# First pooling layer: the 16-column sums in fp32 on GpSimd instead of matmuls; sample states through array tiles and one longer stream

## The chip, the cores and the metric

One Trainium2 chip, 8 cores, the same program on each: every core takes one prompt of the batch and 16 of the 128 sample sequences. There is no communication between cores. The metric is the device time of the slowest core in microseconds.

## The reference, cut to what matters

One step of a two-layer trunk, layer 0 with a pooling mixer and layer 1 with a retention mixer, each followed by a SwiGLU FFN (D_MODEL 1024, D_FF 2816), over 2064 prompt positions (16 meta tokens and 2048) and one new token for each sample.

```python
# layer 0, four groups of 256 channels, windows w = 2, 4, 8, 16
s = cs[:, end, sl] - cs[:, start, sl]          # sum over the trailing w rows
diff = (s / cnt - xn).astype(xn.dtype)
mixed = einsum('btgc,gcd->btgd', diff, w_pool) * pool_scale
# layer 1, sample group, one token: for each of 4 heads, state (256, 512)
s_new = gamma * s0 + k^T v
o = q s_new                                    # then GroupNorm, gate, w_out
```

The new states of the samples (16 samples x 4 heads x 256 x 512 fp32 a core, 32 MB) are read from and written to HBM.

## The kernel before

Activations lie with channels on the partitions and tokens along the free dimension. The tokens are done in two halves: half 0 has 1056 columns (16 samples, 16 meta tokens, 1024 prompt tokens) in tile `hA`, half 1 has 1024 columns (and the 16 sample columns, carried over) in `hB`. A column block is 352 wide (`BW`); the first pooling layer works in four blocks, `FIRST`, of 176, 176, 352 and 352 columns, whose inputs are loaded one after the other (each load waits for the one before, the last for the first FFN weights too).

The stages in order of time: pooling layer of half 0 (`p0_*`), FFN 0 of half 0, retention layer of half 0 (`ret_layer(0)`), FFN 1 of half 0, FFN 0 of half 1, retention layer of half 1, FFN 1 of half 1. The second pooling layer (`p1_steps`) and the recurrent states of the samples (`sample_steps`) are no stages of their own: they are "streams" (`S.add`), lists of steps that are put between the steps of a main stage in proportion to its cost. `S.finish` puts in what is left of a stream. In the program before, heads 0 and 1 of the samples are a stream of FFN 1 of half 0, heads 2 and 3 of FFN 0 of half 1.

**Order on each engine.** The program order gives the dependences (through keys of tiles and PSUM banks). A planner (`Prog.arrange`) then puts the operations of each engine in an order by list scheduling with a cost for each operation, and each engine runs its order strictly. The four PSUM banks `pb` are a ring handed out in program order, so an operation that gets a bank in the program waits until the one four banks before has been read out, wherever the planner would like it. `sx`, `po` and the two banks of `psU` are outside the ring.

**The first pooling layer, `p0_block(b)`** (L713, the line of all matmuls; L722 `tensor_tensor`; L725 `scalar_tensor_tensor` on VectorE; L729 copies and L733 activations on ScalarE). `p0_x` writes the normalised input in bf16 (`hB`), eight VectorE instructions. `p0_group` sums a window of w columns by w matmuls a channel tile, each with an identity times 1/w (the first with 1/w - 1) and the input shifted by k columns, all into one `pb` bank; ScalarE copies it out. `p0_out` multiplies with the pooling weights and adds to `hA`. Then the norm of FFN 0 follows, and its first matmuls, `pb<-xn,wring`, take the next banks of the ring.

**The samples, a unit for each sample and head.** `U` has four slots of 128 x 1024 fp32, one state each. `unit_a` loads the state of two units ahead (DMA on the SP queue), spreads the sample's row of v over 128 partitions by a matmul with the selector `sel` (`psU<-vx,sel`), and adds k v to the state with two VectorE instructions. `unit_b` casts the state to bf16 (`snb`, ScalarE), scales it by gamma in place (ScalarE), stores it (SP queue), and multiplies the cast state of the unit before with the masked q (`po<-snb,qm`, two matmuls of 128 stationary columns, of which 16 matter). After 16 units the head's output is normalised and gated.

**Weights** come by DMAs from the GpSimd queue (L157, `wring`), with a wait for each where its ring space is not yet free; the first five each wait for the one before.

**The retention layer** computes q, k, v (`main_qkv`) and the gate (`main_g`) head by head, with the recurrent chunks of a head as a stream beside (`chunk_steps`), which use `U`, `psU`, `po` and `sx` too.

## Time and profile before

| | |
|---|---|
| device time, three runs | 1668.44, 1672.44, 1797.84 us (median 1672.44) |
| the profiled execution | 1670.36 us |
| its span, slowest core (core 4) | 1668.8 us |
| spans of the eight cores | 1657.7 to 1668.8 us |
| granted TensorE clock, eight cores | 0.992 to 0.996 |
| busy: TensorE, VectorE, ScalarE, GpSimd | 1620.6, 868.1, 669.9, 542.3 us |
| moved by DMA | 201.31 MB, 121 GB/s over the span |

All times of the prediction's argument are of the one profiled execution. The span is from the first to the last instruction of the slowest core; the device time of the same execution is 1.6 us longer.

### The profile page before, as it was taken

What the parts mean: (1) busy time and instruction counts of PE and PEld (TensorE: products, weight loads), DVE (VectorE), ACT (ScalarE), POOL (GpSimd) and SP (SyncE); (2) the same over time, 40 slices, a digit from 0 to 9 for tenths busy, and PEclk for the clock granted to TensorE, in tenths of its full rate; (3) what the DMA queues carried; (4) which work ended last, traced back from release to release, by engine and by line L of the source; (5) the groups of instructions that cost most, each with busy time, mean ns of one, the idle gap of its engine ahead of it and who ended that gap; (6) DMA issues with size and microseconds to landing.
All of it is one profiled execution on the core that took longest, in us unless ns stands there. A gap on an engine that the chain in (4) does not pass through costs nothing.

```text
span 1668.8 us, 32601 instructions; the slowest of 8 cores (1657.7 to 1668.8 us)
## 1 busy us (share of the span) xinstructions
PE 1620.6 (97%) x10945; PEld 1038.4 (62%) x10945; DVE 868.1 (52%) x1651; ACT 669.9 (40%) x1165; POOL 542.3 (32%) x830
## 2 busy tenths in 40 slices
PE   6999999999999999999999999999999999999997
PEld 5666666555565665666665665665655656666666
DVE  4622222855655663889283354448556566422225
ACT  4621022354433554544373544555543345310123
POOL 3000001557747631222140210025677475000002
PEclk9999999999999999999999999999999999999999
DMA  6634434243235466686678987976443241543422
GB/s 156 157 52 85 83 67 82 52 77 64 39 64 102 77 160 176 181 217 158 159 196 209 242 215 213 246 199 190 77 102 59 58 100 27 114 76 56 91 46 103
DMA packets 55745, 201.31 MB, mean 121 GB/s; under 512 B 6688, under 2 KB 21024, under 8 KB 45840
## 3 DMA queue, kind: packets, MB, share of 16 engines
q0 software_dynamic: 15840, 103.82, 35.4%
q1 hardware_dynamic: 39600, 95.07, 16.5%
q8 instruction: 92, 1.51, 0.4%
q14 instruction: 69, 0.57, 0.1%
q10 hardware_dynamic: 144, 0.35, 0.1%
HBM read 256.69 MB, written 47.25 MB: 182 GB/s over the span
## 4 chain that ended last, share of the span: by engine, by line
PE 87%; DMA 5%; issue 2%; ACT 2%; POOL 2%; DVE 2%; DVEq 0%; POOLq 0%; ACTq 0%; SPq 0%
PE pb L713 78%; PE po L713 4%; DMA U<-sret 3%; PE psU L713 2%; PE sx L713 2%; PE sx L717 1%; DMA hB<-xT 1%; DMA nrs<-U 1%; ACT rstd L733 0%; POOL hC L722 0%; DMA cf_sb<-cf 0%; DVE xn L725 0%; POOL aff L722 0%; POOL stt L722 0%; ACT L733 0%
## 5 line engine op out<-in xcount | busy, mean ns | idle before, releaser
L713 PE MATMUL pb<-xn,wring 128*128 128x352 bf16 (+3 forms) x5856 | 936.3, 308 | 12.0 <-ACT sg L733 7.0
L713 PEld LDWEIGHTS pb<-xn,wring 128*128 128x128 bf16 x5856 | 564.5, 98 | 308.0 <-issue 19.1
L713 PE MATMUL pb<-hC,wring 128*128 128x352 bf16 (+4 forms) x2576 | 425.4, 307 | 1.2 <-DVE hB L722 1.2
L722 DVE TENSOR_TENSOR hC<-pb,sg 128x352 bf16<-128x352 f32 (+3 forms) x270 | 136.5, 508 | 373.0 <-PE pb L713 346.9
L713 PEld LDWEIGHTS pb<-hC,wring 128*128 128x128 bf16 x2576 | 249.6, 98 | 124.3 <-issue 2.0
L733 ACT ACTIVATE sg<-pb 128x352 bf16<-128x352 f32 (+3 forms) x270 | 120.4, 451 | 461.7 <-PE pb L713 452.2
L713 PE MATMUL pb<-wring,xn 128*128 128x512 bf16 (+1 forms) x544 | 163.2, 379 | 0.0
L157 POOL DMA_DIRECT2D wring<-w_gu x44 | 24.5, 556 | 418.0 <-PE pb L713 389.0
L722 DVE TENSOR_TENSOR hB<-pb,hB 128x352 f32<-128x352 f32 (+4 forms) x152 | 73.8, 495 | 95.0 <-PE pb L713 94.0
L725 DVE SCALAR_TENSOR_TENSOR U<-psU,ksf,U 128x512 f32<-128x512 f32 x128 | 94.9, 747 | 21.3 <-DMA U<-sret 9.1
L722 DVE TENSOR_TENSOR hA<-pb,hA 128x352 f32<-128x352 f32 (+1 forms) x144 | 72.7, 513 | 63.9 <-PE pb L713 63.2
L729 ACT CAST snb<-U 128x1024 bf16<-128x1024 f32 x64 | 66.5, 1039 | 79.0 <-DVE U L725 55.9
L725 DVE SCALAR_TENSOR_TENSOR U<-U,psU 128x1024 f32<-128x1024 f32 x64 | 78.0, 1218 | 30.4 <-PE psU L713 19.9
L713 PEld LDWEIGHTS pb<-wring,xn 128*128 128x128 bf16 (+1 forms) x544 | 51.8, 98 | 50.3 <-issue 6.4
L722 POOL TENSOR_TENSOR aff<-aff,cf_sb 128x512 f32<-128x512 f32 (+1 forms) x68 | 67.5, 993 | 47.7 <-DVE aff L722 43.5
L722 POOL TENSOR_TENSOR accb<-accb,sq 128x352 f32<-128x352 f32 (+1 forms) x72 | 62.4, 867 | 62.3 <-ACT sq L733 46.2
L729 ACT CAST U<-U 128x1024 bf16<-128x1024 f32 x64 | 66.7, 1042 | 39.3 <-DVE U L725 29.9
L1194 ACT ACTIVATE on<-po,stt 128x512 bf16<-128x512 f32 (+1 forms) x68 | 52.8, 777 | 71.7 <-POOL stt L1188 38.4
L157 POOL DMA_DIRECT2D wring<-w_d x32 | 17.3, 541 | 178.2 <-PE pb L713 178.2
L733 ACT ACTIVATE U<-U 128x1024 f32<-128x1024 f32 x64 | 67.6, 1056 | 5.7 <-ACT snb L729 0.4
L722 DVE TENSOR_TENSOR aff<-sx,cf_sb 128x512 f32<-128x512 bf16 (+1 forms) x68 | 45.0, 662 | 38.7 <-PE sx L717 23.4
L1183 DVE BATCH_NORM_STATS2 stt<-po 128x6 f32<-128x512 f32 (+1 forms) x68 | 47.3, 695 | 27.0 <-PE po L713 23.6
(147 smaller groups left out, 1703.4 us busy)
## 6 DMA issues: line engine op xcount, KB each, us to landing
wring<-w_gu POOLq DMA_DIRECT2D x44, 1024.0 KB, 10.2
U<-sret SPq DMA_DIRECT2D x64, 512.0 KB, 5.9
nrs<-U SPq DMA_DIRECT2D x64, 512.0 KB, 5.5
wring<-w_in POOLq DMA_DIRECT2D x24, 1024.0 KB, 9.7
wring<-w_d POOLq DMA_DIRECT2D x16, 768.0 KB, 7.8
wring<-w_d POOLq DMA_DIRECT2D x16, 640.0 KB, 10.4
wring<-w_out POOLq DMA_DIRECT2D x8, 1024.0 KB, 10.6
hA<-xT SPq DMA_DIRECT2D x2, 1408.0 KB, 13.9
```

What stands on the lines that cost most here:

```text
L157: h.dma_start(out=o_ap, in_=i_ap).then_inc(sem, 16)
L713: return P.op('pe', lambda h: h.matmul(out, lhsT=lhsT, rhs=rhs, start=start, stop=stop), reads=reads, writes=writes, cost=passes * max(_fr ...
L717: return P.op('pe', lambda h: h.transpose(out, in_, ident), reads=reads, writes=writes, cost=max(_free(out), 64) / 2.4 + 1.3)
L722: return P.op(eng, lambda h: h.tensor_tensor(out=out, in0=a, in1=b, op=op), reads=reads, writes=writes, cost=cost)
L725: return P.op('dve', lambda h: h.scalar_tensor_tensor(out=out, in0=a, scalar=s, in1=b, op0=op0, op1=op1), reads=reads, writes=writes, cost ...
L729: return P.op('act', lambda h: h.copy(out=out, in_=in_), reads=reads, writes=writes, cost=130 + 0.93 * _free(out))
L733: return P.op('act', lambda h: h.activation(out=out, in_=in_, func=func, bias=bias, scale=scale), reads=reads, writes=writes, cost=160 + 0 ...
L1183: dve(lambda h: h.bn_stats(out=s[0:n, 0:6], in_=po[0:n, :]), [pok], [sk], 690)
L1194: act(lambda h: h.activation(out=on[0:n, :], in_=po[0:n, :], func=ACT.Identity, bias=s[0:n, 9:10], scale=s[0:n, 8:9]), [pok, sk], [onk], 777)
```

## The change

1. In the first pooling layer, the group with window 16 (channel tiles 6 and 7) no longer goes through matmuls. Its normalised input is kept in fp32 in scratch tiles `XF` (which share the memory of the rotary table `cs`), with 16 columns of the block before in front, copied by GpSimd. GpSimd sums by doubling, four additions a tile (steps 1, 2, 4, 8), and VectorE forms sum/16 minus input. The two tiles share the scratch `XF[2]` and `XF[3]`.
2. As `cs` is scratch at first, its load moves from behind the input loads to behind the pooling layer.
3. The sample units go in pairs and fours. v's row is also copied to partitions 32 to 63 (one more ScalarE copy a head), and one operation of the tensor engine spreads two samples with two matmuls of 32 rows each, in two row tiles of the array. The output is formed for four samples at once by eight matmuls of 32 stationary columns, in four column tiles. `snb` has four buffers for it; the selector `sel` and its GpSimd instruction are gone. The GroupNorm of the samples then runs over 128 partitions, and its transposes over 128 columns in place of 16.
4. The stream of the samples starts beside head 3 of the first retention layer (four units, of which the states lie in `hC`), and the remaining 60 units are one stream over both FFNs and the q, k, v step of head 0 of the second retention layer.

```diff
@@ first pooling layer (G_SUM is 3)
-            for c in range(8):
+            for c in range(2 * G_SUM):
                 stt(B.b(c, 0, c0, n), A.f(c, c0, n), ...)
+            for c in range(2 * G_SUM, 8):
+                X, xkk = XF[c - 6], [('XF', c - 6)]
+                x0 = 0
+                if b:
+                    m = FIRST[b - 1][1] - (32 if b == 1 else 0)
+                    pcopy(X[:, 0:16], X[:, m:m + 16], xkk, xkk)
+                    x0 = 16
+                stt(X[:, x0:x0 + n], A.f(c, c0, n), w32[...], r[:, o:o + n], ALU.mult, ALU.mult, ..., xkk)
...
+                if g >= G_SUM:
+                    X, xkk = XF[c - 6], [('XF', c - 6)]
+                    src, sk, sh = X, xkk, 1
+                    while sh < w:
+                        i = 2 if src is X or src is XF[3] else 3
+                        dst, dk = XF[i], [('XF', i)]
+                        lo = 2 * sh
+                        tt('pool', dst[:, lo:16 + n], src[:, lo:16 + n], src[:, lo - sh:16 + n - sh], ALU.add, sk, dk)
+                        src, sk = dst, dk
+                        sh *= 2
+                    stt(B.b(c, 1, c0, n), src[:, 16:16 + n], 1.0 / w, X[:, 16:16 + n], ALU.mult, ALU.subtract, ...)
+                    continue
@@ the load of cs: from behind the input loads to behind the pooling layer
-        csl = P.dma('sp', [(cs[:, 0, :], csd[0, :, 0:NA]), ...], semkey='cs', after=xl[3:4])
...
         wrel(wprec)
+        P.dma('sp', [(cs[:, 0, :], csd[0, :, 0:NA]), ...], writes=csk, semkey='cs')
@@ samples, two units
+                        if (h, b) != (0, 2):
+                            s_load(16 * h + b + 2 + i)
+                    def spread(e):
+                        for i in range(2):
+                            p = slice(32 * i, 32 * i + 32)
+                            ins = e.matmul(psU[:, i, :], lhsT=identb[p, 32*i+b+i:32*i+b+i+1].to_broadcast([32, 128]),
+                                           rhs=vx[h][p, :], start=True, stop=True)
+                    P.op('pe', spread, ..., cost=290)
@@ samples, four units
+                        for c in range(2):
+                            for j in range(4):
+                                w0 = 17 * (b + j) - b // 4
+                                ins = e.matmul(po[32 * j:32 * j + 32, :], lhsT=qm[:, c, w0:w0 + 32], rhs=snb[j][:, c, :],
+                                               start=b == 0 and c == 0, stop=b == 12 and c == 1)
+                    P.op('pe', dots, ..., cost=650)
@@ v of the samples, twice
                     acopy(o[0:n, :], pb[0:n, :], [pk], ok)
+                    if t == 8:
+                        acopy(o[n:2 * n, :], pb[0:n, :], [pk], ok)
@@ the streams
+        first4, sw = sw[0:7], sw[7:]
+        ret_layer(0, A, 'R0', 32, NA, norm_after(A, C_NF1, 'F01'), first4)
...
-        s01 = S.add(sample_steps(0, True) + sample_steps(1, False), 0.97 * fcost)
+        ss = S.add(sw, 2 * fcost + 8 * 8 * NB + 8 * 8 * 512)
...
-        s23 = S.add(sample_steps(2, False) + sample_steps(3, False), 0.97 * fcost)
...
+        ret_layer(1, B, 'R1', 0, NY, norm_after(B, C_NF1, 'F11'), ss)
@@ in ret_layer
             main_qkv(0)
+            if half == 1:
+                S.finish(beside)
...
+                side = S.add(beside, 2.2 * span) if h == 3 and half == 0 else None
                 main_g(h)
+                if side:
+                    S.finish(side)
```

## Rows read from the trace of the kernel before

**Rows 1.** The page: busy time, share of the span, instructions.
```profile
PE 1620.6 (97%) x10945; PEld 1038.4 (62%) x10945; DVE 868.1 (52%) x1651; ACT 669.9 (40%) x1165; POOL 542.3 (32%) x830
```
**Rows 2.** Windows by stage: length, busy us (instructions) by engine, clock, DMA share, GB/s.
```profile
0.00:100.00 100.00, 82.62 (x667) 62.60 (x668) 54.59 (x128) 48.11 (x126) 19.96 (x42) 0.97 0.57 131
100.00:310.00 210.00, 210.00 (x1410) 137.68 (x1409) 60.87 (x113) 39.40 (x83) 24.79 (x36) 1.00 0.41 74
...
866.00:1128.00 262.00, 252.81 (x1670) 163.05 (x1669) 123.56 (x225) 130.46 (x182) 33.18 (x51) 0.99 0.86 218
```
**Rows 3.** Windows of 10 us in which the tensor engine stands idle or slow.
```profile
880.00:890.00 10.00, 7.84 (x51) 4.70 (x48) 2.90 (x5) 1.34 (x3) 0.00 (x0) 1.00 0.99 281
...
1000.00:1010.00 10.00, 6.39 (x32) 3.34 (x31) 4.10 (x7) 3.87 (x4) 0.00 (x0) 0.83 0.89 294
...
1040.00:1050.00 10.00, 7.51 (x51) 4.38 (x49) 4.11 (x10) 9.15 (x12) 1.80 (x5) 1.00 0.84 255
1050.00:1060.00 10.00, 10.00 (x58) 6.22 (x57) 7.05 (x14) 6.32 (x8) 1.19 (x2) 0.83 0.90 211
```
**Rows 4.** Timeline, VectorE then TensorE, 1000 to 1007 us: start, us, instruction, idle before.
```profile
1004.25 2.26 DVE L725 SCALAR_TENSOR_TENSOR U<-psU,ksf,U 128x512 f32<-128x512 f32 x3 [3.68 <-DMA U<-sret]
...
1006.00 0.58 PE L713 MATMUL psU<-vx,sel 128*128 128x512 bf16 x1 [3.61 <-DVE U L725]
```
**Rows 5.** Groups by shape, TensorE: the matmuls that the change removes or replaces.
```profile
L713 PE MATMUL po<-snb,qm 128*128 128x512 bf16 x128 | 43.0, 383 | 0.2 <-ACT on L1194 0.2
L713 PE MATMUL psU<-vx,sel 128*128 128x512 bf16 x64 | 24.1, 384 | 3.6 <-DVE U L725 3.6
L713 PE MATMUL pb<-hB,snb 128*128 128x352 bf16 x120 | 22.4, 325 | 0.4 <-DVE hB L725 0.2
```
**Rows 6.** Timeline, TensorE: unbroken runs of 352 and of 512 columns.
```profile
105.74 19.55 PE L713 MATMUL pb<-xn,wring 128*128 128x352 bf16 x130
...
325.43 2.54 PE L713 MATMUL pb<-wring,xn 128*128 128x512 bf16 x11
327.80 0.31 PE L713 MATMUL pb<-xn,wring 128*128 128x352 bf16 x1
```
**Rows 7.** Timeline, TensorE, 366 to 369 us: stationary tiles of 32 between 128 columns.
```profile
366.70 1.04 PE L713 MATMUL pb<-wring,xn 128*32 128x512 bf16 x4
367.67 0.39 PE L713 MATMUL po<-hC,U 128*128 128x512 bf16 x1
367.99 0.71 PE L713 MATMUL pb<-wring,xn 128*32 128x512 bf16 x2
368.54 0.38 PE L713 MATMUL po<-U 128*128 128x512 bf16 x1
368.76 0.39 PE L717 MATMUL sx<-identb,on 128*128 128x128 bf16 x4
369.07 0.71 PE L713 MATMUL pb<-wring,xn 128*32 128x512 bf16 x2
```
**Rows 8.** Timeline, GpSimd, first 60 us.
```profile
35.73 0.59 POOL L157 DMA_DIRECT2D wring<-w_gu  x1 [13.00 <-DMA wring<-w_gu]
36.74 0.76 POOL L722 TENSOR_TENSOR xn<-hA 128x352 bf16<-128x352 f32 x1 [0.42 <-DMA hA<-xT]
46.53 0.59 POOL L157 DMA_DIRECT2D wring<-w_gu  x1 [9.03 <-DMA wring<-w_gu]
49.42 1.13 POOL L722 TENSOR_TENSOR xn<-hA 128x352 bf16<-128x352 f32 x1 [2.30 <-DMA hA<-xT]
```
**Rows 9.** Timeline, VectorE, 57 to 75 us: last block's input and last residual additions.
```profile
57.20 0.58 DVE L725 SCALAR_TENSOR_TENSOR hB<-hA,w,rstd 128x352 bf16<-128x352 f32 x1
...
72.85 1.08 DVE L725 SCALAR_TENSOR_TENSOR hA<-pb,cf_sb,hA 128x352 f32<-128x352 f32 x2 [1.95 <-PE pb L713]
```
**Rows 10.** Timeline, TensorE: the first FFN matmuls.
```profile
70.80 0.24 PE L713 MATMUL pb<-xn,wring 128*128 128x176 bf16 x1
```
**Rows 11.** Groups by shape, GpSimd: fp32 additions.
```profile
L722 POOL TENSOR_TENSOR accb<-accb,sq 128x352 f32<-128x352 f32 x48 | 42.2, 879 | 50.8 <-ACT sq L733 41.5 <-ACT accb L733 5.5 <-ACT snb L729 0.4
```
**Rows 12.** DMA issues, 866 to 1128 us: count, KB each, median us to landing.
```profile
U<-sret SPq DMA_DIRECT2D x33, 512.0 KB, 6.9
nrs<-U SPq DMA_DIRECT2D x33, 512.0 KB, 6.4
```

176 lines of the change are left out of this document (95 added, 81 removed).

## The prediction

> **What bounds the kernel now.** First the page's busy line: the tensor engine is busy for 1620.6 us of 1668.8, so it bounds nearly everywhere, and some 48 us are left in which it stands idle [rows 1]. Then the windows by stage, to see where those are: 17.4 us of them in the first 100 us, none in the FFN that follows, 9.2 us in the FFN of the second half [rows 2]. A change can therefore gain in two ways: matmul time that is taken away where the engine is never short of work, or a wait that goes. Time taken away where it waits for something else gains nothing.
>
> What the engine waits for differs by stage. In the second half's FFN the windows of 10 us show it at 7.84, 6.39 and 7.51 us busy, while the DMA engines are 0.84 to 0.99 busy, and twice a clock of 0.83 [rows 3]; the granted clock has two levels, 2.4 and 1.2 GHz, and a mean of 0.83 is a third of the window at the lower one, which costs half of that, 1.7 us. Idle and clock together are 2.2 + 3.6 + 1.7 + 2.5 + 1.7 = 11.7 us. The timeline names the cause of the largest: VectorE waits 3.68 us for a state of a sample (`U<-sret`), and the tensor engine, which must run its order, stands behind it for 3.61 us before it may spread the next v [rows 4].
>
> The first 70 us are another thing. The last input block is there at 49.4 us, where GpSimd starts on it [rows 8]; its normalised input begins at 57.2 us, and its last residual additions end at 73.9 us [rows 9]. The FFN's matmuls begin at 70.8 us [rows 10], though their first weights landed at 35.7 us, where GpSimd's wait for them ends [rows 8]: the ring of four `pb` banks holds them back until the last banks of the pooling layer are read out. So FFN matmuls cannot fill holes in the pooling layer, and what matters is the end of the last block's chain.
>
> **The window sums.** Removed are 64 matmuls of 352 columns (blocks 2 and 3), 32 of 176 and 32 of 144. An unbroken run gives the pace: 130 of 352 columns in 19.55 us, 0.149 us each [rows 6]; by columns the small ones cost 0.075 and 0.061. The sum is 9.5 + 2.4 + 2.0 = 13.9 us of tensor engine time, and eight ScalarE copies. (The group's mean of 325 ns [rows 5] contains the pipeline's depth and is not a price.) That is the upper end, if nothing new stands in the way.
>
> Something does. In their place stand, a block, eight dependent GpSimd additions. The trace has the same addition at 128x352 in fp32 for 0.88 us [rows 11]; the same shape of product took 0.76 us once and 1.13 us beside busy engines [rows 8]. With about 0.13 us between dependent instructions a chain of eight is 8.1 us, by 1.13 us 10.1. For block 3: input at about 56.7 us (in the old order 57.2, first of the eight now), chain to 65.5 with the copies in front, 1.1 us more for the halo's two instructions on the same queue, two VectorE instructions of 0.6 us partly beside it, then two pairs of matmuls and two additions, 2 us: about 69 us where before it was 73.9. Meanwhile the tensor engine has 28 window matmuls (4.2 us) and the other groups' outputs, and the ring lets through only the FFN step whose banks come before group 3. Gain 5 us. Block 2 needs no more: its chain starts at 44 us and ends before block 3's input is normalised. Bounds: 9 us gained if the chain ends at 65 because the additions take 0.76 us, and 5 us lost if GpSimd's queue is held (a rival, below).
>
> The Trainium skill speaks against this step: "GPSIMD Engine Reference", section Engine selection, says elementwise additions on a tile belong on VectorE and cost about twice as much on GpSimd; VectorE, a little over half busy there, would by that rule do the chain in about 4 us and end some 3 us earlier. The sum above does not use it.
>
> **The load of `cs`** (1 MB) leaves the DMA engines free from 49 to 59 us, where only weights for later steps come in, and lies afterwards in a stage with DMA share 0.41 in which the tensor engine has no idle time [rows 2]. It is read 200 us later. Nothing.
>
> **The samples' array tiles.** Before, a unit has one matmul of 512 columns to spread v and two for the output, 192 in all [rows 5]. Their pace is (327.80 - 325.43) / 11 = 0.216 us [rows 6], so they cost 41.5 us. They lie among the FFNs' matmuls, where the engine is otherwise busy, so a saving counts in full. After, there are 32 pairs and 16 operations of eight. If tiles run side by side, a pair lasts 0.216 us and the eight two times 0.216. No row shows two tiles together. But rows show what it costs to go to a narrower tile and back: four matmuls with 32 stationary columns occupy 366.70 to 367.67, that is 0.97 us in place of 4 x 0.216 = 0.86; the one of 128 columns behind them 0.32 in place of 0.22; the next two 0.55 in place of 0.43 [rows 7]. Each change of tile shape costs 0.11 us, 0.22 for in and out again. And the matmuls of a group can hardly start at the same moment: four transposes behind one another start in (0.31 - 0.11) / 4 = 0.05 us steps [rows 7]. So a pair costs 0.216 + 0.22 = 0.44, with one step 0.49, I take 0.46; the eight cost 0.43 + 0.22 = 0.65, with three steps 0.80, I take 0.72. Sum: 32 x 0.46 + 16 x 0.72 = 14.7 + 11.5 = 26.2 us, a gain of 15.3 us. Lower price 24.5 (gain 17), higher 28.5 (gain 13); with changes of shape hidden 13.8 (gain 27.7); with tiles one after the other 64 x 0.216 + 128 x 0.216 + 48 x 0.22 = 52.1, a loss of 10.6.
>
> That a change of tiling mode drains the engine is what the Trainium skill says in "TensorEngine Tiling (Array Packing)", Key Properties; the trace agrees, with 0.11 us. "TensorE: Matmul & The Clock Gate", Part 3, reports four row tiles with K = 32 at 3.07 times one after another, not 4; by that the eight would cost 8 x 0.216 / 3.07 = 0.56 us and the change of shape, which is inside my two ends.
>
> **The longer stream.** In the second half's FFN 33 units are loaded and 33 stored [rows 12]. The new stream has 60 units over 1,179,648 columns of work, of which an FFN has 540,672, so 27.5 units fall into each FFN, four into the retention layer before and five into the q, k, v step after. That takes 5.5 loads and stores of 0.5 MB, 5.5 to 6 MB, from a stage that moves 218 GB/s x 262 us = 57 MB, and puts them where the DMA engines are less busy. A tenth less traffic, and 9 us of distance a unit in place of 8. Every unit still has the same four slots and loads come only two units ahead, so the delays get rarer and don't vanish: I take half of the 11.7 us, 6, with bounds 0 and 11.7.
>
> **What is added.** Four ScalarE copies, hidden beside q, k, v; 16 transposes of 128 columns for 16 of 16, at 0.05 us steps under 1 us; four units beside head 3 in the first retention layer, where the chunks share `psU`; five units beside the rotary products, and the load of head 0's state, which now waits for a sample's store. VectorE and ScalarE are half busy [rows 1], the queues behind them have other matmuls to cover. I put 2 us on all of it, bounds 0 and 6.
>
> **Sum.** -5 - 15.3 - 6 + 2 = -24.3 us. Against the profiled execution 1670.36 - 24.3 = 1646.1, its span 1644.5; the median of the runs is 2.1 us above it, so **1648 us**.
>
> **Rivals.**
> - **GpSimd is held by the weights.** Its queue runs in order, and in this stretch it stood 13.0 and 9.0 us for a weight DMA before issuing the next [rows 8]. The planner estimates the landing; if it puts additions of blocks 1 or 2 behind such an issue, they end at 46.5 or later and all outputs, and by the ring of banks the next block, move. For: the waits are there today. Against: the additions are critical and ready earlier, so they should be put in front. Price: the last block ends 5 us later than before instead of 5 earlier, 1658 us.
> - **The tiles don't run side by side.** The groups then cost 52.1 us: -5 + 10.6 - 6 + 2 = +1.6, **1674 us**, slower than before. It decides from the point where the groups cost more than 41.5 + 9 = 50.5 us, 3.2 us for four units; half overlap isn't enough for it. For: no row shows two tiles at once. Against: the tiles are disjoint in the array and write disjoint banks or partitions.
> - **The late states go altogether**: 11.7 instead of 6, and the lower price of the tiles: -5 - 17 - 11.7 + 2 = -31.7, 1641 us. For: the busiest stage is relieved. Against: the same slots and distance.
> - **Changes of shape are hidden** behind other matmuls: -5 - 27.7 - 6 + 2 = -36.7, 1636 us. Against: in rows 7 each one shows.
>
> **How the numbers follow.** Chances: forecast 0.50 (own range 1641 to 1656), held GpSimd 0.20, late states gone 0.14, hidden changes of shape 0.07, serial tiles 0.09. The range 1632 to 1664 leaves out the serial tiles and the ends of others. Within 2% means 1639 to 1706 us, about what a measurement of this kernel can tell from no change. Below lie the hidden changes of shape and a part of the late-states case and of the forecast with the prologue's upper bound: 0.19 faster. Slower by over 2% needs several losses together: 0.03. The same: 0.78.
>
> **What the changed profile would show.** Right: `po` matmuls with 32 stationary columns whose eight take 0.65 to 0.8 us until the next 128-column matmul starts; `psU` pairs 0.44 to 0.49; the first FFN matmul at 66 to 69 us and the last pooling addition near 69; fewer idle windows from 866 to 1060; no new idle time in the retention layers. Wrong: GpSimd additions behind a weight issue of 10 us, the first FFN matmul after 71 us, eight `po` matmuls over 1.7 us, or a tensor engine that waits for `XF` sums with its clock at half for longer than before.

## The result and the profile after

| | before | changed |
|---|---|---|
| device time, median (range) | 1670.76 us (4 runs) | 1646.72 us (1644.68 to 1764.9, 4 runs) |
| ratio | 1 | 0.9855, 95% interval [0.9836, 0.9875] |
| span of the profiled execution | 1668.8 us | 1643.8 us (core 4, as before) |

The 1764.9 us is an execution in which the cores of one die had a lower clock, and it is not in the ratio. The change gives 24 us, 1.5%: within the 2% band, and 1 us from the 1648 predicted. The sum was right; how it is made up was not (the errors of its terms cancelled), and most of what follows is about that.

The page's busy line of the changed kernel:

```profile
PE 1589.3 (97%) x10817; PEld 1010.3 (61%) x10817; DVE 881.9 (54%) x1671; ACT 663.3 (40%) x1157; POOL 561.9 (34%) x867
```

Its windows by stage (columns as in [rows 2]):

```profile
0.00:100.00 100.00, 74.72 (x555) 53.44 (x556) 65.37 (x138) 45.90 (x119) 40.15 (x79) 0.97 0.57 131
...
866.00:1128.00 262.00, 256.77 (x1759) 163.29 (x1758) 136.55 (x251) 126.33 (x186) 47.50 (x67) 0.99 0.88 222
```

Against [rows 1] the tensor engine is busy for 31.3 us less (1620.6 to 1589.3); the 13.9 us of window matmuls and the 18.1 us worked out below make 32.0. Against [rows 2] its idle time in the first 100 us rose from 17.4 to 25.3 us, while VectorE went from 54.59 to 65.37 us busy: of 13.9 us of window matmuls 7.9 came back as waiting. From 866 to 1128 us the idle time fell from 9.2 to 5.2 us.

**The pooling layer.** Timeline of the changed kernel, GpSimd, the last block's sums:

```profile
60.33 4.23 POOL L721 TENSOR_TENSOR cs_sb<-cs_sb 128x366 f32<-128x366 f32 x4 [0.44 <-DVE cs_sb L724]
65.09 0.82 POOL L721 TENSOR_TENSOR cs_sb<-cs_sb 128x366 f32<-128x366 f32 x1 [0.53 <-DVE cs_sb L724]
67.18 2.81 POOL L721 TENSOR_TENSOR cs_sb<-cs_sb 128x364 f32<-128x364 f32 x3 [1.27 <-DVE hB L724]
```

VectorE, its last residual additions:

```profile
71.26 1.08 DVE L724 SCALAR_TENSOR_TENSOR hA<-pb,cf_sb,hA 128x352 f32<-128x352 f32 x2
```

TensorE, the first FFN matmul ([rows 10]):

```profile
68.30 0.24 PE L712 MATMUL pb<-xn,wring 128*128 128x176 bf16 x1 [0.17 <-issue]
```

Eight additions take from 60.33 to 69.99 us, 9.7 us. By themselves they are as priced, 0.89 us each in the mean and 0.14 us apart; but twice the chain waits for VectorE (1.27 us for the instruction that reads a scratch tile before it may be overwritten, 0.53 for the next product). The last residual additions end at 72.3 us, where [rows 9] has 73.9.

What became of VectorE shows in the groups by shape, first 110 us (instructions, busy us, mean ns, idle time). The kernel before:

```profile
L725 DVE SCALAR_TENSOR_TENSOR hB<-hA,w,rstd 128x352 bf16<-128x352 f32 x16 | 8.3, 580 | 2.5 <-ACT rstd L733 2.5
```

The changed kernel:

```profile
L724 DVE SCALAR_TENSOR_TENSOR hB<-hA,w,rstd 128x352 bf16<-128x352 f32 x12 | 10.5, 910 | 0.0
...
L724 DVE SCALAR_TENSOR_TENSOR cs_sb<-hA,w,rstd 128x352 f32<-128x352 f32 x4 | 3.5, 879 | 0.2 <-ACT rstd L732 0.2
...
L724 DVE SCALAR_TENSOR_TENSOR hA<-pb,cf_sb,hA 128x352 f32<-128x352 f32 x16 | 8.6, 574 | 0.1
```

The product of two SBUF inputs went from 580 to 910 ns; the addition of the same size whose first input is PSUM stayed (582 ns before, 574 now). The mean of 910 ns hides what happens to each. Timeline, VectorE: a product with no addition beside it, and two that start in one:

```profile
42.64 0.58 DVE L724 SCALAR_TENSOR_TENSOR cs_sb<-hA,w,rstd 128x352 f32<-128x352 f32 x1 [0.21 <-ACT rstd L732]
...
61.09 0.62 DVE L724 SCALAR_TENSOR_TENSOR hB<-hA,w,rstd 128x352 bf16<-128x352 f32 x1
61.63 1.11 DVE L724 SCALAR_TENSOR_TENSOR hB<-hA,w,rstd 128x352 bf16<-128x352 f32 x1
```

GpSimd, the additions in which they start:

```profile
60.33 0.99 POOL L721 TENSOR_TENSOR cs_sb<-cs_sb 128x366 f32<-128x366 f32 x1 [0.44 <-DVE cs_sb L724]
61.47 0.89 POOL L721 TENSOR_TENSOR cs_sb<-cs_sb 128x364 f32<-128x364 f32 x1
```

The first of the two starts late in its addition and takes 0.62 us, the second early in its own and takes 1.11; both end 0.38 us after the addition does. In the single records the same holds, at 0.38 us, for all twelve products of the last two blocks that start inside an instruction of GpSimd with SBUF inputs (durations from 0.62 to 1.26), while the four that start in none take 0.57 to 0.59. So such a product gets nowhere until the addition is done. In windows of 10 us VectorE is by then full (7.30 and 7.62 busy before):

```profile
45.00:55.00 10.00, 7.77 (x38) 3.84 (x36) 10.00 (x14) 5.19 (x13) 6.91 (x9) 0.83 0.96 233
55.00:65.00 10.00, 8.50 (x50) 4.22 (x50) 9.93 (x18) 6.43 (x15) 5.54 (x8) 1.00 0.39 69
```

**The tiles.** Timeline of the changed kernel, TensorE, a group of eight output matmuls and what follows:

```profile
710.65 0.62 PE L1311 MATMUL po<-snb,qm 128*32 128x512 bf16 x8
711.20 1.17 PE L712 MATMUL pb<-hC,wring 128*128 128x320 bf16 x7
```

The second four of these eight:

```profile
710.87 0.39 PE L1311 MATMUL po<-snb,qm 128*32 128x512 bf16 x4
```

The same, a pair that spreads v:

```profile
657.59 0.39 PE L1273 MATMUL psU<-vx,identb 32*128 32x512 bf16 x2
657.91 0.46 PE L712 MATMUL pb<-xn,wring 128*128 128x320 bf16 x2
```

Eight matmuls of 512 columns in 0.55 us, two in 0.32, from start to the next one's start. On the way in each costs 0.09 us more: the matmul of 320 columns ahead of it started 0.23 us before it (at 710.42 and at 657.36), where the step between two such is 0.14 (657.22 to 657.36). In sum that is 0.64 and 0.41 us, where one after another they would take 1.73 and 0.43 by the pace of [rows 6]. The second four start 0.22 us behind the first, which is the pace of a single matmul, and the last four take 0.32 us until the next shape starts, 0.10 of it for the change. In the single records the matmuls of a group of four start 3 to 4 ns apart in most cases; the steps of 0.05 us that the prediction took over from transposes aren't there. For all: 16 x 0.64 + 32 x 0.41 = 23.4 us in place of 41.5, 18.1 us of work saved.

**The stream.** DMA issues of the changed kernel, 866 to 1128 us ([rows 12]):

```profile
U<-sret SPq DMA_DIRECT2D x33, 512.0 KB, 8.2
nrs<-U SPq DMA_DIRECT2D x32, 512.0 KB, 7.1
```

Timeline, TensorE, its longest wait for a state's `psU` there ([rows 4]):

```profile
988.18 0.61 PE L1273 MATMUL psU<-vx,identb 32*128 32x512 bf16 x2 [2.45 <-DVE U L724]
```

As many loads and one store less, and DMA share 0.88 as against 0.86. But this is a window of time and not the stage: the FFN 0 of half 1 ends at 1138 us before and at 1108 us now (its last `pb<-hC,wring`, core 4), so that the window now holds a part of the q, k, v step as well. Counted by the stage (871 to 1138 us before, 862 to 1108 us now) there are 31 loads and 30 stores in place of 35 and 34, and 54.2 MB in place of 59.0. The stage has also become 21 us shorter, so the DMA share is 0.88 as against 0.86 and the rate 220 as against 221 GB/s: less is moved, in less time. The longest such wait shrank from 3.61 to 2.45 us.

### The profile page after: what moved, and what is told of

Same layout as the page of the kernel before. It is cut to its first block, busy times and chain, and to the rows that moved or that the text cites. A ratio compares the mean times of both kernels' runs of the same rounds, so it can differ in the third digit from the quotient of the medians.

```text
span 1643.8 us, 32354 instructions; the slowest of 8 cores (1630.2 to 1643.8 us)
## 1 busy us (share of the span) xinstructions
PE 1589.3 (97%) x10817; PEld 1010.3 (61%) x10817; DVE 881.9 (54%) x1671; ACT 663.3 (40%) x1157; POOL 561.9 (34%) x867
## 4 chain that ended last, share of the span: by engine, by line
PE 87%; DMA 5%; DVE 4%; issue 2%; ACT 2%; POOL 1%; DVEq 0%; POOLq 0%; SPq 0%; ACTq 0%
PE pb L712 78%; PE po L712 3%; PE sx L712 2%; PE psU L712 2%; PE sx L716 1%; DMA hA<-xT 1%; DMA U<-sret 1%; DMA hB<-xT 1%; DVE xn L724 1%; DVE hB L724 1%; DMA nrs<-U 1%; PE psU L1273 1%; DVE hA L721 1%; POOL hC L721 0%; ACT L732 0%
## 5 line engine op out<-in xcount | busy, mean ns | idle before, releaser
L712 PE MATMUL pb<-xn,wring 128*128 128x352 bf16 (+3 forms) x5856 | 915.1, 308 | 7.8 <-ACT sg L732 4.5
L712 PE MATMUL pb<-hC,wring 128*128 128x352 bf16 (+4 forms) x2576 | 412.8, 307 | 1.2 <-DVE hB L721 1.2
L712 PE MATMUL pb<-wring,xn 128*128 128x512 bf16 (+1 forms) x544 | 156.0, 379 | 0.0
L724 DVE SCALAR_TENSOR_TENSOR U<-psU,ksf,U 128x512 f32<-128x512 f32 x120 | 89.0, 746 | 19.3 <-PE psU L1273 8.9
L1214 ACT ACTIVATE on<-po,stt 128x512 bf16<-128x512 f32 x68 | 52.8, 777 | 82.6 <-POOL stt L1208 56.5
L728 ACT CAST snb<-U 128x1024 bf16<-128x1024 f32 x60 | 62.3, 1039 | 53.7 <-DVE U L724 41.2
L1203 DVE BATCH_NORM_STATS2 stt<-po 128x6 f32<-128x512 f32 x68 | 47.3, 696 | 38.9 <-PE po L712 20.9
L732 ACT ACTIVATE U<-U 128x1024 f32<-128x1024 f32 x60 | 63.3, 1056 | 4.7
## 6 DMA issues: line engine op xcount, KB each, us to landing
wring<-w_in POOLq DMA_DIRECT2D x24, 1024.0 KB, 10.5
wring<-w_out POOLq DMA_DIRECT2D x8, 1024.0 KB, 10.5
hA<-xT SPq DMA_DIRECT2D x2, 1408.0 KB, 11.6
```

Source lines behind the costliest of these rows:

```text
L712: return P.op('pe', lambda h: h.matmul(out, lhsT=lhsT, rhs=rhs, start=start, stop=stop), reads=reads, writes=writes, cost=passes * max(_fr ...
L724: return P.op('dve', lambda h: h.scalar_tensor_tensor(out=out, in0=a, scalar=s, in1=b, op0=op0, op1=op1), reads=reads, writes=writes, cost ...
L728: return P.op('act', lambda h: h.copy(out=out, in_=in_), reads=reads, writes=writes, cost=130 + 0.93 * _free(out))
L732: return P.op('act', lambda h: h.activation(out=out, in_=in_, func=func, bias=bias, scale=scale), reads=reads, writes=writes, cost=160 + 0 ...
L1203: dve(lambda h: h.bn_stats(out=s[0:n, 0:6], in_=po[0:n, :]), [pok], [sk], 690)
L1214: act(lambda h: h.activation(out=on[0:n, :], in_=po[0:n, :], func=ACT.Identity, bias=s[0:n, 9:10], scale=s[0:n, 8:9]), [pok, sk], [onk], 777)
```

## The experiments

All ratios are to the kernel before on the same chip, with 95% intervals; the chips differ between groups of runs. From each profile I also read two numbers on all eight cores: when GpSimd issues the fifth FFN weight (the FFN's first matmul lies 38.5 to 40.4 us before it on the eight cores of before, changed, e5, e6, e7 and e9, so this is the pooling layer's end plus nearly a constant), and what is left of that core's span behind it. Medians over the eight cores:

| kernel | ratio | fifth weight, us | the rest, us |
|---|---|---|---|
| before | 1 | 108.5 | 1554.4 |
| before, other order (r3) | 0.9983 [0.9966, 0.9999] | 108.5 | 1551.5 |
| changed | 0.9855 [0.9836, 0.9875] | 106.2 | 1532.2 |
| changed again (r1) | 0.9880 [0.9855, 0.9905] | 105.0 | 1534.2 |
| changed, other order (r2) | 0.9871 [0.9849, 0.9892] | 104.6 | 1531.5 |
| sums alone (e9) | 0.9986 [0.9973, 0.9999] | 104.8 | 1553.4 |
| sums and tiles, old streams (e2) | 0.9945 [0.9925, 0.9966] | 104.9 | 1550.8 |
| sums and long stream, full matmuls (e3) | 0.9900 [0.9865, 0.9936] | 105.1 | 1545.9 |
| all, but serial tiles (e4) | 0.9938 [0.9915, 0.9961] | 103.0 | 1552.5 |
| tiles and stream, matmul sums (e1) | 0.9940 [0.9921, 0.9959] | 115.0 | 1536.2 |
| the same, `cs` load at its old place (e6) | 0.9939 [0.9923, 0.9955] | 117.2 | 1535.7 |
| sums on VectorE (e5) | 0.9947 [0.9925, 0.9969] | 110.2 | 1542.5 |
| one tile on GpSimd (e7) | 0.9872 [0.9857, 0.9888] | 112.0 | 1529.0 |
| squares on ScalarE (e8) | 0.9892 [0.9870, 0.9913] | 105.5 | 1540.7 |

### e1: the sums as matmuls again

```diff
-        G_SUM = 3
+        G_SUM = 4
```

> The changed kernel with its first part undone: the window of 16 goes through matmuls again, tiles and stream stay. Theory (the sums are worth what the first 110 us show, where the fifth FFN weight is issued at 107.9 us after the change and at 110.3 before): 2.4 us slower than the changed kernel, 1649 us, and that weight issued near 110.3 us. Rival (all 13.9 us of removed matmul time count somewhere): 1660 us. Second rival (the sums on GpSimd cost as much as they give): 1647 us.

Measured: 0.9940, fifth weight at 115.0 us. By the ratio that is 1661 us, the first rival's time, but it is no clean undo. Without scratch tiles nothing holds the late `cs` load back, and it was issued on SP's queue at 1.57 us, ahead of `sp_prev` and the second input block. Timeline of e1, TensorE:

```profile
19.27 6.98 PE L712 MATMUL po<-cf_sb,hC 128*128 128x16 f32 x32 [4.48 <-DMA hC<-sp_prev]
```

What follows: a megabyte put in front of the inputs costs a wait of 4.5 us; of the sums it tells nothing that can be separated.

### e2: the old two streams, with pairs and tiles

```diff
-        ss = S.add(sw, 2 * fcost + 8 * 8 * NB + 8 * 8 * 512)
+        s01 = S.add(sample_steps(0, True) + sample_steps(1, False), 0.97 * fcost)
...
+        s23 = S.add(sample_steps(2, False) + sample_steps(3, False), 0.97 * fcost)
```

> The changed kernel with its last part undone: the samples are two streams again, heads 0 and 1 in FFN 1 of half 0, heads 2 and 3 in FFN 0 of half 1, in pairs and with array tiles as changed. Theory (the longer stream is worth the idle and slow-clock time that went between 606 and 1128 us, 14.6 - 13.6 us of idle time and 3.4 us of clock): 4 us slower than the changed kernel, 1651 us, with idle windows and a clock under 1.00 back around 880 to 1060 us. Rival (those went because units go in pairs, and the stream's length does nothing): 1647 us. Second rival (the work put beside the retention layers costs more than it gives): 1644 us or less.

Measured: 0.9945, a loss well over the 4 us expected. The stalls that I expected to come back before 1128 us are the smaller part of it (on core 3 the idle time from 606 to 1128 us is 15.2 us as against 11.6 in the changed kernel, by the windows below). Timeline of e2, TensorE, core 3, the end of the second stream:

```profile
1143.11 1.05 PE L1305 MATMUL po<-snb,qm 128*32 128x512 bf16 x8 [5.07 <-ACT snb L728]
1147.83 0.59 PE L716 MATMUL sx<-identb,on 128*128 128x128 bf16 x4 [3.67 <-ACT on L1214]
```

The same place in e9:

```profile
1136.48 3.48 PE L1304 MATMUL po<-snb,qm 128*128 128x512 bf16 x8 [2.56 <-ACT snb L728]
1143.60 0.25 PE L716 MATMUL sx<-identb,on 16*128 16x16 bf16 x4 [3.63 <-ACT on L1214]
```

A stream that must be done at the FFN's end shows its tail: the last four states' casts, the group norm, the transposes and the gate come one behind the other, and nothing else is left to run. Before, with single units, TensorE was idle for 3.7 us from 1128 to 1405 us on core 3; e9, which differs there by the grouping, has 10.5.

### e3: matmuls 128 wide, with the new stream

```diff
-                                w0 = 17 * (b + j) - b // 4
-                                ins = e.matmul(po[32 * j:32 * j + 32, :], lhsT=qm[:, c, w0:w0 + 32], rhs=snb[j][:, c, :],
+                                w0 = 16 * (b + j)
+                                ins = e.matmul(po[:, :], lhsT=qm[:, c, w0:w0 + 128], rhs=snb[j][:, c, :],
```

> The changed kernel with full-width matmuls for the samples: a pair is spread by two matmuls over all 128 rows, four samples' outputs by eight matmuls of 128 stationary columns, at the same places. Theory (tiles count in full): 41.4 us of matmuls for 23.3 us, 18 us slower, 1665 us. Rival (the engine has slack where they lie, or more overlaps than the tensor engine alone): less than 10 us slower, under 1657 us.

### e4: the same shapes in one tile

```diff
-                                ins = e.matmul(po[32 * j:32 * j + 32, :], lhsT=qm[:, c, w0:w0 + 32], rhs=snb[j][:, c, :],
+                                ins = e.matmul(po[0:32, :], lhsT=qm[:, c, w0:w0 + 32], rhs=snb[j][:, c, :],
```

> The changed kernel with the same tile shapes, but all matmuls of a group in the same tile of the array: both of a pair in rows 0 to 31, all eight of the output in columns 0 to 31. Theory (the gain is that tiles run side by side, and shape changes cost 0.1 us): a pair takes 0.41 + 0.22 = 0.63 us, eight take 8 x 0.216 + 0.2 = 1.94 in place of 0.64, together 32 x 0.22 + 16 x 1.3 = 27.8 us slower than the changed kernel, 1674 us, slower than the kernel before all changes. Rival (a narrow matmul is cheaper by itself): 1647 to 1660 us.

Measured: e3 0.9900, e4 0.9938. Timeline of e4, TensorE, core 3:

```profile
711.30 1.90 PE L1311 MATMUL po<-snb,qm 128*32 128x512 bf16 x8
713.14 2.14 PE L712 MATMUL pb<-hC,wring 128*128 128x320 bf16 x14
```

In one tile the eight take 1.84 us, in four tiles 0.55; a pair 0.53 (657.88 to 658.41) as against 0.32. That is 16 x 1.29 + 32 x 0.21 = 27.4 us more TensorE work, the 27.8 of the expectation; yet the kernel is only 0.9938 - 0.9869 = 0.0069 slower than the changed one (mean of its three ratios), 11.5 us. With e3 it is 18.1 us more work (the price of 41.5 less 23.4) and 0.0031, 5 us, with an uncertainty about as large. So tiles do run side by side, and less than half of what they save reaches the end: e3 meets its rival (under 10 us slower) and e4 has the time of its rival, though not its reason, since a narrow matmul in one tile isn't cheaper. Where it goes is seen in windows over the two FFNs with the states and over the retention layer behind them, on core 3 of each kernel. (The windows are the same in time; in a faster kernel the last part of each already belongs to the next stage.) Before:

```profile
606.00:1128.00 522.00, 510.77 (x3401) 331.20 (x3400) 304.36 (x565) 262.30 (x390) 108.60 (x184) 0.99 0.82 203
1128.00:1405.00 277.00, 273.34 (x1814) 164.11 (x1812) 172.88 (x325) 129.64 (x213) 183.78 (x271) 1.00 0.40 84
```

Changed:

```profile
606.00:1128.00 522.00, 510.44 (x3519) 327.38 (x3518) 317.40 (x591) 251.63 (x389) 122.05 (x198) 1.00 0.79 197
1128.00:1405.00 277.00, 272.93 (x1834) 164.31 (x1833) 168.99 (x325) 137.08 (x221) 170.46 (x257) 1.00 0.41 90
```

e3:

```profile
606.00:1128.00 522.00, 519.12 (x3470) 337.63 (x3471) 314.18 (x577) 249.23 (x383) 114.49 (x193) 1.00 0.79 198
1128.00:1405.00 277.00, 274.58 (x1844) 168.15 (x1843) 169.12 (x323) 130.67 (x213) 173.28 (x260) 1.00 0.39 81
```

e4, the first of the two:

```profile
606.00:1128.00 522.00, 514.46 (x3406) 324.52 (x3404) 305.96 (x556) 243.38 (x379) 112.95 (x190) 1.00 0.78 193
```

e9:

```profile
606.00:1128.00 522.00, 516.73 (x3456) 335.41 (x3455) 317.45 (x581) 265.45 (x395) 114.04 (x190) 1.00 0.82 206
1128.00:1405.00 277.00, 266.50 (x1760) 160.11 (x1757) 162.57 (x312) 125.63 (x207) 173.06 (x259) 0.98 0.34 72
```

e2:

```profile
606.00:1128.00 522.00, 506.82 (x3474) 323.04 (x3472) 318.44 (x592) 258.56 (x394) 116.93 (x194) 0.99 0.81 204
1128.00:1405.00 277.00, 261.92 (x1734) 157.51 (x1732) 160.89 (x308) 126.53 (x205) 173.73 (x260) 0.97 0.37 82
```

Window less busy is idle. In both stages together: before 14.9 us, changed 15.6, e3 5.3, e9 15.8, e2 30.3. From e3 to the changed kernel tiles take 18.1 us of work away and 10.3 of them come back as idle time; with the old streams (e9 to e2) 14.5 do. (Over the eight cores e3 has 5.3 to 11.7 us, median 8.6, and the changed kernel 13.0 to 18.0, median 15.6.) From before to changed the idle time stays as it was, but only as a balance: the longer stream by itself takes 10.5 us of it away (e9 to e3), and the tiles bring 10.3 back.

What TensorE waits for then, core 3, 606 to 1128 us (us in total, times, longest). The changed kernel:

```profile
PE pb L712 <- ACT sg L732: 3.7, 3, 2.1
PE sx L712 <- DVE dfb L724: 3.0, 2, 1.9
...
PE psU L1273 <- DVE U L724: 1.1, 1, 1.1
```

e3:

```profile
PE sx L712 <- DVE hB L724: 1.4, 1, 1.4
...
PE pb L712 <- ACT sg L732: 0.2, 1, 0.2
```

Only 1.1 us is for a state (1.1 to 3.2 on cores 0, 1, 5 and 7). The rest is for the FFN's own activation (`sg`, ScalarE) and for instructions of VectorE for the second pooling layer (`dfb`) and the FFN. So the time comes back as waits for ScalarE and VectorE, which do the FFN's work and the states' in one queue each; which of their instructions make these late no run shows.

### r1, r2, r3: the changed kernel again, and both in another order

The planner breaks ties by a seed; r2 and r3 have another.

```diff
-default_rng(1)
+default_rng(2)
```

> The changed kernel as it is, beside the next ones on one chip. The four kernels before it each undid one part and lost 7.5 to 15 us by their ratios, 51 us in all, where all parts together gained 24. Theory A (the planner's order is worth several us, and each undoing also lost a good order): ratio 0.985 again, about 1647 us. Theory B (the comparison was off by the chip): a ratio of 0.990 or more here.

> The changed kernel with another seed of the planner's random rounds and nothing else: the same instructions in another order on each engine. Theory A (order is worth several us): 5 to 12 us slower than the changed kernel, ratio 0.988 to 0.993. Theory B (the parts are worth what their undoing cost): ratio within 0.002 of the changed kernel's.

> The kernel before with another seed of the planner's random rounds and nothing else. Theory A: differs from the kernel before by 3 to 12 us in either direction (ratio 0.993 to 1.007, outside 0.998 to 1.002). Theory B: ratio 0.998 to 1.002.

Measured: 0.9880, 0.9871, 0.9983. r1 lies between its two theories; r2 and r3 met theory B. The same kernel on another chip moved by 0.0025, 4 us, and another order by a seed by no more than that (r3 by 0.0017, 3 us). A seed doesn't explain that the undos e1, e2 and e3 together lose 30 us of a gain of 22. No undo was run with another seed.

### e5: the doubling sums on VectorE

```diff
-                        tt('pool', dst[:, lo:16 + n], src[:, lo:16 + n], src[:, lo - sh:16 + n - sh], ALU.add, sk, dk)
+                        tt('dve', dst[:, lo:16 + n], src[:, lo:16 + n], src[:, lo - sh:16 + n - sh], ALU.add, sk, dk)
```

> The changed kernel with the doubling sums on VectorE in place of GpSimd. Beside the GpSimd sums VectorE's products of two SBUF inputs took 0.91 us where they take 0.58 alone, while those with a PSUM input stayed at 0.57, and VectorE is 96 to 100% busy from 35 to 65 us: the first layer is now bound by VectorE. Theory (the two engines share access to SBUF): those products go back to 0.58 us, some 9 us of VectorE time in the first 110 us, against 32 additions there of 0.25 to 0.52 us, 13 us: the fifth FFN weight is issued within 2 us of 107.9. Rival (the length of the chain on GpSimd bounds, not VectorE): the chain of a block shrinks from 9.6 to about 4.5 us and that weight is issued 4 us earlier, near 104. The whole within the uncertainty of the planner's order.

Measured: 0.9947, fifth weight at 110.2, 4 to 6 us later than with GpSimd. On core 4 it is at 111.4: neither the theory's 107.9 nor the rival's 104, since an addition takes 0.52 to 0.59 us at these widths and not 0.25 to 0.52. Groups by shape of e5, VectorE, first 110 us:

```profile
L724 DVE SCALAR_TENSOR_TENSOR hB<-hA,w,rstd 128x352 bf16<-128x352 f32 x12 | 6.9, 614 | 0.0
...
L721 DVE TENSOR_TENSOR cs_sb<-cs_sb 128x364 f32<-128x364 f32 x4 | 2.4, 594 | 0.2
```

A window of e5:

```profile
55.00:65.00 10.00, 7.08 (x41) 3.43 (x40) 9.79 (x20) 6.31 (x15) 2.30 (x5) 1.00 0.88 206
```

Two things follow. The stretching of the products (0.91 us) is due to the additions on GpSimd: with the same products and no such additions there it is 0.61. And an addition is in fact quicker on VectorE (0.52 to 0.59 us in the means by shape, as against 0.84 to 0.99 on GpSimd in the changed kernel), but VectorE has no room for it. (The rest of the run is 8 to 11 us longer than in the changed kernel, in stages that the edit doesn't touch; of that below, at e8.)

### e6: matmul sums, and the `cs` load at its old place

```diff
-        G_SUM = 3
+        G_SUM = 4
...
+        csl = P.dma('sp', [(cs[:, 0, :], csd[0, :, 0:NA]), (cs[:, 1, :], csd[1, :, 0:NA])], writes=[('XF', i) for i in range(5)],
+                    semkey='cs', after=xl[3:4])
```

> The changed kernel with the window sums of 16 again as matmuls AND the load of cs back at its old place on SP's queue (behind the fourth input block). e1 had left that load free and it was issued at 1.6 us, in front of the second input block. Theory A (the sums gave about 2.4 us, as the fifth weight issue 110.3 -> 107.9 says, and the rest of e1's loss was the place of the cs load): the fifth FFN weight is issued at 110.3 again, no 4.5 us wait for sp_prev, and the time is 2 to 4 us over the changed kernel, a ratio to before of about 0.988 to 0.990. Rival B (the sums are worth all that e1 showed, 10 us): fifth weight issue after 112, ratio 0.993 or more. Rival C (the cs load's traffic beside the last input block matters too): ratio 0.990 to 0.992 with the last input block later than in the changed kernel.

Measured: 0.9939, fifth weight at 117.2 us, though the pooling layer is now that of before, which ends 8.7 us earlier. Theory A's numbers are missed and rival B's weight is met. But the timeline of e6 (TensorE, core 4) shows what was not foreseen:

```profile
36.32 2.51 PE L712 MATMUL sx<-xn,onesb 128*128 128x352 bf16 x8 [5.14 <-ACT rstd L732]
```

The order that was planned for e6 puts the statistics of the third input block at 36 us, in front of 20 window matmuls of the second block; in before they come at 39.5, behind them. So the wait for the block is bare. It is 4.5 to 6.9 us on the eight cores, where before has 1.1, and explains 3 to 6 of the 8.7 us; the rest is open. e6 is not the pooling layer of before in another setting, and its loss is no clean price of the sums.

### e7: one of the two tiles on GpSimd

```diff
-            for c in range(2 * G_SUM):
+            for c in range(7):
...
-                if g >= G_SUM:
+                if c == 7:
```

> The changed kernel, with only one of the two tiles of window 16 (tile 7) summed on GpSimd; tile 6 goes back to matmuls. GpSimd's chain for the last block is then four additions of about 0.9 us and not eight, 4 to 5 us of 9.6; TensorE gets back 7 us of matmuls in a stretch where it stands idle for 25 us. Theory A (the prologue is bound by VectorE, whose products are stretched from 0.58 to 0.91 us beside the additions, and by the chain behind them): products of hB at 128x352 fall to about 0.75 us in the mean, VectorE 45 to 65 us is under 9.6 of 10 us busy, the fifth weight issue comes at 105 to 106.5 instead of 107.9, and the whole is 1 to 3 us faster. Rival B (TensorE is by then the bound, its matmuls cost in full): the fifth weight issue comes at 109 to 112, halfway back to before. Rival C (nothing changes, the end is set by the last input block's arrival): 107.9 and the same time.

Measured: 0.9872, as the changed kernel. The products of `hB` are back at 608 ns and VectorE at 6.8 to 8.1 of 10 us from 45 to 65, so theory A's cause was right; the gain isn't there. On four cores the fifth weight comes at 108.3 to 109.5, on the other four at 114.5 to 116.2, and these have e6's wait, 2.9 to 7.3 us of it (timeline, TensorE, core 0):

```profile
38.38 2.50 PE L712 MATMUL sx<-xn,onesb 128*128 128x352 bf16 x8 [6.03 <-ACT xn L732]
```

### e8: squares of the first norm on ScalarE

```diff
-                square(A, c, c0, n, ('act', 'dve', 'act', 'pool', 'act', 'dve', 'act', 'dve')[c])
+                square(A, c, c0, n, ('act', 'act', 'act', 'act', 'act', 'dve', 'act', 'act')[c])
```

> The changed kernel, with the squares of the first norm of tiles 1, 3 and 7 on ScalarE (before: VectorE, GpSimd, VectorE), 4 blocks, 12 instructions of which VectorE loses 8 of 0.51 us and GpSimd 4 of 0.9. Theory A (VectorE is the bound of the pooling layer and GpSimd's square of the last block waits behind additions, 52.95 instead of 49.42): VectorE ends about 1 us a block earlier, the square of the last block no longer waits, and the fifth weight issue comes at 105 to 107 instead of 107.9. Rival B (ScalarE, 6.4 to 7 of 10 us busy there, takes over: the seven squares of a block one after another at about 0.5 us delay the root that every product needs): fifth weight issue at 108.5 to 110. Either is 1 to 3 us of the whole.

Measured: 0.9892, fifth weight at 105.5. On core 4 it came 1.7 us earlier than in the changed kernel (106.17 as against 107.91), which is theory A's mark; over the cores it is 0.7. The rest of the run is 6 to 9 us longer, in a part that the edit doesn't touch. Timeline of e8, VectorE, core 4:

```profile
878.89 0.75 DVE L724 SCALAR_TENSOR_TENSOR U<-psU,ksf,U 128x512 f32<-128x512 f32 x1 [8.56 <-DMA U<-sret]
```

TensorE stands 5.5 us behind it. The order of SP's queue differs there from the changed kernel's; that which state comes late is a matter of the whole plan is my reading, and no run separates it from the edit.

### e9: the sums alone

Edits of e2 and e3 together: only the window sums, the late `cs` load and the grouping in pairs and fours are left of the change.

> The window sums on GpSimd (and the late cs load) alone: the samples' matmuls 128 wide as before, and their stream in two parts beside the two halves' FFNs as before, with four snb tiles and pairs kept. TensorE work is that of before less 13.9 us of window sums. Theory A (the sums are worth what the prologue shows, 2.4 us, and the rest of what the undos lost is the planner's order around them, e6's wait of 5.1 us for a root among it): fifth weight issue at 107.5 to 110, ratio to before 0.997 to 1.000. Rival B (the sums are worth 8 to 12 us, as e6 says, in which they were undone): ratio 0.993 to 0.995, with the fifth weight issue at 105 or earlier or a shift that comes in a later stage. Rival C (each part alone gives nothing, since what it frees turns to idle time elsewhere): ratio over 1.000, with the gain of the first 100 us, if there is one, lost again as idle time between 606 and 1405.

Measured: 0.9986 [0.9973, 0.9999], 2.3 us, fifth weight at 104.8. Theory A said 2.4; the fifth weight of core 4, at 106.6, lies between its range and rival B's. Its pooling layer ends 3.7 us earlier than that of before on the median core; the stall at the end of the second stream (shown above) takes a part of it back, as rival C had it. Added to the kernel before, the sums (with the grouping) give 2 to 4 us; taken out of the changed kernel (e6) they cost 12. The bare wait, 3 to 6 us longer than in the kernel before, is a part of these 12. That the rest is the price of e6's order too is likely, since the rest of the run is only 2 to 4 us longer and the pooling layer does what it did before in 8.7 us more, but it isn't shown: no other order of e6 was run.

No version that was run beats the changed kernel.

**The parts as a sum.** With e9, e2, e3 and the changed kernel (0.9869, mean of three) there is a square of tiles and stream, both with the sums. Of 1672 us:

| | old streams | long stream | the stream gives |
|---|---|---|---|
| full matmuls | 0.9986 | 0.9900 | 14 us |
| array tiles | 0.9945 | 0.9869 | 13 us |
| the tiles give | 7 us | 5 us | both: 20 us |

Each difference is uncertain by some 4 to 6 us. 2 + 20 us is the 22 of the mean of the three. Within that, each gives as much alone as beside the other: tiles 7 us without the long stream and 5 with it, neither near the 18.1 us of work that they save.

The lengths of the stages in the profiled executions say the same and show where. Medians of cores 0 to 3 in us, each stage taken to its last `pb<-hC,wring` matmul:

| kernel | FFN 1 of half 0 | FFN 0 of half 1 | retention layer | the three |
|---|---|---|---|---|
| before | 265.1 | 264.4 | 184.9 | 712.7 |
| e9 | 261.7 | 256.0 | 197.1 | 714.3 |
| e2 | 262.4 | 247.1 | 199.7 | 709.6 |
| e3 | 260.9 | 253.4 | 184.8 | 700.0 |
| changed | 257.7 | 242.6 | 189.6 | 690.1 |

(r1 and r2 have 693.8 and 691.3 for the three.) By this the tiles give 5 us with the old streams and 6 to 10 with the long one, the stream 14 and 16 to 20. From before to e9 both FFNs get shorter, by 12 us, and the retention layer gets 12 us longer: in pairs and fours the units delay the FFNs less (TensorE waits 1.0 us for states from 606 to 1128 us on core 3, before 2.4) and leave a longer tail. From e9 to e3 the long stream takes that tail away again.

## Why the prediction was right, and where it was not

**The sum.** Predicted -24.3 us, measured -24 in the runs of the first table and -22 in the mean of the changed kernel's three ratios. The terms for sums, tiles and stream were -5, -15.3 and -6 and came out as some -2.4, -5 to -7 and -13 to -14. That the sum is right is luck.

**The window sums** (-5, bounds -9 to +5; measured -2.4 on the profiled core, -2 to -4 over all). The chain was put at 8.1 us and took 9.7, the difference being two waits for VectorE; its start was put at about 57 and was 60.3, since block 3's products of `XF` come at 59.60 and 63.69. The step that failed is the one that gave VectorE's instructions their old durations ("two VectorE instructions of 0.6 us partly beside it", input at 56.7): beside GpSimd's additions a product of two SBUF inputs takes 0.91 us in the mean and up to 1.26, and VectorE, a little over half busy in the mean of the run but already 7.2 to 7.6 of 10 us from 35 to 65 us in the kernel before, is full from 45 to 65 us. The mark "last pooling addition near 69" was wrong (72.3); "first FFN matmul at 66 to 69" held at its edge (68.3). The Trainium skill has this in "SBUF — State Buffer", section SBUF: two separate sides: it names, as what contends, a GpSimd instruction with a VectorE instruction that is in a 2-port mode or has two SBUF inputs, the latter only where GpSimd's reads SBUF. The trace agrees, by 580 to 910 ns for the products of two SBUF inputs and 582 to 574 for the additions with one from PSUM. The same section says that the one that comes second fully blocks. The trace agrees here too, not by the mean, which mixes blocked and free products, but by the single rows: a product that starts inside an addition ends 0.38 us after it, whether it started 0.16 or 0.76 us into it.

**VectorE as a rule would have it.** The additions on VectorE, which the prediction weighed and left out of its sum, were run as e5. The Trainium skill's "GPSIMD Engine Reference", section Engine selection, calls an addition about twice as slow on GpSimd. The runs agree in the direction, with 0.84 to 0.99 us as against 0.52 to 0.59. But the pooling layer ends 4 to 6 us later than in the changed kernel, because the engine was no longer half empty (9.79 of 10 us busy from 55 to 65).

**The tiles** (-15.3). Their price was nearly right and a little high, since it had steps of 0.05 us between starts that aren't there: 0.41 and 0.64 us as against 0.46 and 0.72 taken (the marks 0.44 to 0.49 and 0.65 to 0.8 are missed from below), 23.4 us as against 26.2; 18.1 us of work saved. The step that failed is "they lie among the FFNs' matmuls, where the engine is otherwise busy, so a saving counts in full". It counts for 5 to 7 us of 18.1, with either stream. The rest comes back as waiting: on core 3 the idle time from 606 to 1405 us rises from 5.3 to 15.6 us, or from 15.8 to 30.3 with the old streams. Most of it, in the changed kernel, is waiting for ScalarE's and VectorE's instructions of the FFN and the second pooling layer, and little for the states themselves. Half busy in the mean, as the prediction had them, these engines don't keep up everywhere.

**The longer stream** (-6, bounds 0 to -11.7; measured -13 to -14, beside the same grouping). Its mechanism was wrong, and the gain lies outside its bounds. Of the 5.5 units that were to leave the stage 4 left, 31 loads in place of 35, but DMA share and rate are no lower. The states' waits there were already shorter with the old streams once the units went in pairs and fours (e9). What the stream gives, as far as the runs show, is that the samples' work need not end with an FFN: e2 and e9 have 15.1 and 10.5 us of idle time from 1128 to 1405 us and the clock at 0.97 and 0.98 there, the changed kernel 4.1 and 1.00. With a part of this it pays for the grouping, which made the tail heavier (before, with single units, had 3.7). The prediction had set 2 us for all added work and no word for the tail. Untested is the long stream with single units, and so what the grouping costs and gives alone.

**Together** tiles, stream and added work were put at -15.3 - 6 + 2 = -19.3, and the square gives -20. This is luck as well. By the windows of core 3 the idle time of both kernels is the same, 14.9 and 15.6 us, as if the work saved had counted in full; but the square shows no such link between the two parts. The tiles' saving came back in large part as waiting whichever stream there was, and the stream took away about as much waiting of another kind.

**The `cs` load** (0). Right: nothing waits for it in its new place. That its place can cost is shown by e1.

**The rivals.** GpSimd held by weights: no. Its issues came later (46.5 to 59.3 us for the third), but no matmul of the FFN waited for them, and from 24.97 to 69.93 us GpSimd stands idle for no more than 0.32 us before such an issue. Serial tiles: no, as the 0.55 us shows; and its price was wrong too, since e4, which has this mechanism, isn't slower than before but 0.6% faster. Late states gone: no, 2.45 us is left of the longest on TensorE, and in e8 VectorE waits 8.56 for one. Changes of shape hidden: no, each shows.

## What to carry to other kernels

Before work is moved to an idle engine, look at its windows where the work will lie and not at its mean, and at what runs beside it: two SBUF inputs on VectorE next to GpSimd additions cost half as much again in the mean. A saving on an engine that is 97% busy needn't count in full: here less than half of it did, and the rest came back as waits for other engines. Where two parts may need each other, test them in a square of four rather than by single undos; here it showed no sign that they do, and that a right sum was made of wrong terms. Count loads and waits by the stage and not by a window of time, since a faster kernel has moved on. Where a planner orders the kernel, look in every undo at what else moved before its difference is read as the price of a part.

## What was unexpected

- Four matmuls in four column tiles of 32 with K = 128 start within some 10 ns of each other and the next four 0.22 us later, so that the tiles run side by side almost fully. With the changes of shape the eight are 8 x 0.216 / 0.64 = 2.7 times as fast as one after another, and a pair in two row tiles only 0.43 / 0.41 = 1.05 times, since a change of shape in and out weighs most where only two matmuls lie between.
- VectorE products with two SBUF inputs beside GpSimd's fp32 additions: 0.91 us in the mean in place of 0.58 at 128x352, 0.98 in e8, and 1.10 to 1.26 for those that start soon after an addition of full width: each ends 0.38 us after the addition in which it starts; GpSimd's additions themselves 0.79 to 1.04 us in the last block, 0.89 in the mean, as against 0.88 in [rows 11].
- The same kernel's pooling layer ends at 101.5 to 109.9 us (as the fifth weight) on the eight cores of one execution, a spread larger than what the change gives there. A reading of this stage on one core alone would have shown almost any gain.
